# Three branch tiles loaded ahead of the gates, and a silu and two VectorE operations placed later, in a single-core decoder step

## What is computed

```python
q, k, v, iq, ik, iw, za, cu, zc, gt = split(x @ w_in)          # w_in: 2048 x 10832
# A: an indexer picks the top keys of each query, then sparse attention over them
sc   = sum_h relu(iq_h @ ik.T) * iw_h ; sel = top_k(sc)
attn = softmax(q @ k[sel].T * DH**-0.5 - slope * dist) @ v[sel]
# B: causal depthwise convolution, 31 taps
c    = depthwise_conv(ga * sigmoid(gb))
a_br = (attn * silu(za)) @ w_att_out                           # 1024 -> 2048
c_br = (silu(layer_norm(c)) * silu(zc)) @ w_conv_out           # 1024 -> 2048
mixed = sigmoid(gt[0]) * a_br + sigmoid(gt[1]) * c_br
y = layer_norm(ALPHA * x + mixed @ w_o)
```

## Time and profile before

| what | us |
|---|---|
| time, median of 3 runs (lowest to highest) | 1519.48 (1519.25 to 1519.65) |
| time of the profiled execution | 1517.25 |
| its span, first to last instruction | 1515.5 |
| PE busy in the span | 1492.2 (98%) |
| ACT / DVE / POOL busy | 888.6 / 680.6 / 668.5 |
| mean granted TensorE clock | 0.996 |

### The profile page before, as it was taken

How to read it: one execution, slowest core, us unless ns; L and a number is a source line. 1 busy time by engine, 2 the same in 40 slices (tenths; PEclk the granted TensorE clock), 3 DMA queues, 4 the chain that set the end, 5 groups by cost and what they waited for, 6 DMA issues and landing times.

```text
span 1515.5 us, 28644 instructions
## 1 busy us (share of the span) xinstructions
PE 1492.2 (98%) x11036; PEld 1166.2 (77%) x11036; DVE 680.6 (45%) x1444; ACT 888.6 (59%) x1218; POOL 668.5 (44%) x665
## 2 busy tenths in 40 slices
PE   9999999989999999999999999999999999999997
PEld 9955677877777877777777777877767777888885
DVE  4244677853241010118888888585123222121028
ACT  5798755656564565665566666769865665221120
POOL 5254433423332343365555565774444444333340
PEclk9999999999999999999999999999999999999999
DMA  7334343322333555633333333324354443732213
GB/s 266 84 89 115 88 121 85 92 80 79 107 100 112 162 144 141 198 96 99 84 84 84 84 88 101 102 57 135 115 154 130 133 147 115 253 122 82 80 60 125
DMA packets 246595, 174.11 MB, mean 115 GB/s; under 512 B 10449, under 2 KB 222897, under 8 KB 245631
## 3 DMA queue, kind: packets, MB, share of 16 engines
q1 hardware_dynamic: 241319, 162.00, 37.2%
q10 hardware_dynamic: 5160, 10.48, 1.9%
HBM read 156.31 MB, written 16.87 MB: 114 GB/s over the span
## 4 chain that ended last, share of the span: by engine, by line
PE 88%; ACT 5%; DVE 2%; POOL 2%; issue 1%; DMA 1%; DVEq 0%; SPq 0%; ACTq 0%
PE ps L1833 54%; PE ps L2207 12%; PE ps L1804 11%; PE ps L1905 3%; PE ps L1971 1%; PE ps L2100 1%; PE ps L1801 1%; ACT whi L958 1%; PE ps L1800 1%; PE ps L2090 1%; ACT scaled L957 1%; ACT squares L940 1%; DVE bias L1477 1%; ACT x L1013 1%; POOL wlo L824 1%
## 5 line engine op out<-in xcount | busy, mean ns | idle before, releaser
L1833 PE MATMUL ps<-x,whi 128*128 128x288 f16 (+2 forms) x4864 | 926.8, 291 | 0.0
L1833 PE MATMUL ps<-x,wlo 128*128 128x288 f16 (+2 forms) x2432 | 707.0, 291 | 0.0
L1833 PEld LDWEIGHTS ps<-x,whi 128*128 128x128 f16 x4864 | 472.0, 98 | 148.8 <-issue 8.4
L824 POOL TENSOR_TENSOR wlo<-scaled,whi 128x1024 f16<-128x1024 f32 x192 | 408.8, 2151 | 317.1 <-ACT whi L958 317.1
L1833 PEld LDWEIGHTS ps<-x,wlo 128*128 128x128 f16 x2432 | 238.1, 98 | 71.5
L957 ACT ACTIVATE scaled<-raw,few 128x1024 f32<-128x1024 f32 x192 | 219.5, 1143 | 20.2 <-POOL few L819 10.5
L958 ACT ACTIVATE whi<-raw,few 128x1024 f16<-128x1024 f32 x192 | 218.5, 1138 | 0.0
L947 ACT ACTIVATE few<-ps 128x1 f32<-128x1 f32 x96 | 16.3, 170 | 338.8 <-PE ps L1844 326.7
L2207 PE MATMUL ps<-b,whi 128*128 128x288 f16 x1024 | 190.1, 287 | 0.0
L940 ACT ACTIVATE squares<-raw 128x2048 bf16<-128x2048 f32 x95 | 180.4, 1898 | 6.2 <-DMA raw<-in_w_conv_out_dram 6.2
L1631 DVE SCALAR_TENSOR_TENSOR ps<-U,dwT,ps 128x512 f32<-128x512 f32 x232 | 175.2, 755 | 0.0
(11 more groups left out here) (308 smaller groups left out, 1485.5 us busy)
## 6 DMA issues: line engine op xcount, KB each, us to landing
raw<-in_w_in_dram SPq DMA_DIRECT2D x82, 1024.0 KB, 5.6
raw<-in_w_o_dram SPq DMA_DIRECT2D x16, 1024.0 KB, 5.0
both_gates<-gates_dram SPq DMA_DIRECT2D x16, 576.0 KB, 6.7
raw<-in_w_att_out_dram SPq DMA_DIRECT2D x16, 512.0 KB, 4.1
raw<-in_w_conv_out_dram SPq DMA_DIRECT2D x16, 512.0 KB, 5.4
gates_dram<-tmp_gate ACTq DMA_DIRECT2D x24, 288.0 KB, 2.1
vpage<-in_cache_v_dram SPq DMA_DIRECT2D x32, 128.0 KB, 2.7
kTs<-in_cache_k_dram SPq DMA_DIRECT2D x64, 64.0 KB, 1.9
```

What stands on the lines that cost most here:

```text
L824: ins = nc.gpsimd.tensor_tensor(wlo16[:, buf, c], scaled[:, c], whi16[:, buf, c], ALU.subtract)
L1833: ins = mm(ps[:, bank + half, 0:width], w[b][:, k, :], x16[:, k, x, t0 + half * width:t0 + (half + 1) * width], start=(k == 0 and m == 0), ...
```

## The change

Three edits, all of order alone; no instruction is added or removed.

- SP: branch tiles are loaded one at a time (`branch_tile(j)`) instead of in pairs. Three of them (0, 1, 2) are issued ahead of the waits for the stored gates and the operands, instead of two. After the gates of pair 0 the order is tile 3, tile 4, gates 1, tile 5, tile 6, gates 2, ..., tile 15, gates 7. So each of gates 1 to 6 now stands behind one more tile.
- POOL: `silu(N_G2 - 1)` stands behind `split_scaled(N_G2 + 1)` instead of ahead of it.
- DVE: the wait for v_hi, the v_lo subtraction and the q_last copy stand behind the four p_lo subtractions of group 0 (s == 1) instead of ahead of the softmax of group 0.

```diff
-            def branch_pair(i):
-                for b in range(2):
-                    n = N_BR + 2 * i + b
-                    buffer_free(n, scaled_only=True)
...
-            branch_pair(0)
+            def branch_tile(j):
+                n = N_BR + j
+                buffer_free(n, scaled_only=True)
+                for c, w in ((0, w_att_out), (1, w_conv_out)):
+                    sp.dma_start(raw[:, n % 2, c * DC:(c + 1) * DC].rearrange("p (k c) -> p k c", k=8),
+                                 w[:, j * P:(j + 1) * P].rearrange("(k p) c -> p k c", p=P)
+                                 ).then_inc(raw_here[n % 2], 16)
+
+            for j in range(3):
+                branch_tile(j)
 
             for s in gate_stored:
                 sp.wait_ge(s, 16 * 16)
...
             sp.wait_ge(xlo_ready, 3 * KC)
             for i in range(8):
                 if i:
-                    branch_pair(i)
+                    branch_tile(2 * i + 1)
+                    if i < 7:
+                        branch_tile(2 * i + 2)
...
-            silu(N_G2 - 1)
             for n in range(N_G2 + 1, N_BR):
                 split_scaled(n, 0.5)
+                if n == N_G2 + 1:
+                    silu(N_G2 - 1)
...
             dve.wait_ge(tile_taken, N_GT - C_OF + 2)
-            nc.vector.tensor_copy(q_last[:, :].rearrange("p (h t) -> p h t", h=HEADS), qT[:, :, 4 * P:LP]
-                                  ).then_inc(q_last_ready, 1)
-            dve.wait_ge(v_hi_ready, 1)
-            nc.vector.tensor_tensor(v_lo[:, :, :], kv[:, 0:4, KVH * DH:], v_hi[:, :, :].bitcast(F32), ALU.subtract
-                                    ).then_inc(v_lo_ready, 1)
             for s in range(GROUPS + 1):
                 if s >= 1:
...
                         nc.vector.tensor_tensor(lo, a, hi.bitcast(F32), ALU.subtract).then_inc(p_lo_ready, 1)
+                    if s == 1:
+                        dve.wait_ge(v_hi_ready, 1)
+                        nc.vector.tensor_tensor(v_lo[:, :, :], kv[:, 0:4, KVH * DH:], v_hi[:, :, :].bitcast(F32),
+                                                ALU.subtract).then_inc(v_lo_ready, 1)
+                        nc.vector.tensor_copy(q_last[:, :].rearrange("p (h t) -> p h t", h=HEADS), qT[:, :, 4 * P:LP]
+                                              ).then_inc(q_last_ready, 1)
                     dve.wait_ge(o_out, s)
```

## The result

| kernel | median us (lowest to highest) | profiled execution / its span | mean clock |
|---|---|---|---|
| before | 1519.47 (1519.25 to 1519.65) | 1517.25 / 1515.5 | 0.996 |
| changed | 1504.26 (1503.93 to 1504.5) | 1504.5 / 1502.7 | 0.998 |

The ratio is 0.9903, with a 95% interval of 0.9889 to 0.9917: 15.2 us less by the medians. I had forecast 1506.4 us, with a range of 1503.5 to 1511. The span of the profiled execution came down by 12.8 us; I had worked out 1502.4 for it.

The account below looks back on a forecast made before the run. PE was taken to bound the kernel, so only its idle time and slow clock could be won: 5.95 + 1.55 + 5.55 = 13.05 us off 1519.48 gives 1506.4 us, range 1503.5 to 1511.

Parts of the forecast that it names:

- What bounds: PE, busy for 1492.2 of 1515.5 us; the change aims at its waits of 4.1, 1.55 and 3.8 us.
- Attention: PE's 4.1 us wait at the transposes goes, with 1.5 us of slow clock and 0.35 at the transposes: 5.95 us.
- v_lo and q_last behind p_lo: On DVE at group 0, both end before they are needed; v_lo has at least 5 us of cover.
- Silu: At gate tile N_G2 + 1, PE's 1.55 us wait ahead of the norm matmul goes, with no clock tail.
- Branch tiles: Behind tile N_BR, PE's 3.8 us wait goes and 1.75 us of slow clock with it: 5.55 us.
- (a): Softmax of group 0 takes over q_last's and v_lo's port waits: 8.2 us saved, 1511.3 us; chance 5%.
- (b): Branch wait returns one tile later, up to 3 us, a long one with 1.75 us tail: 1508 to 1511; chance 9%.
- (c): Gates 1 to 6 land after DVE wants them, at all six pairs: slower, 1523.2 us; chance 2%.
- (d): PE's idle time turns up elsewhere in pieces, so under 3 us are won: 1517 us; chance 3%.
- the slow clock behind the two long waits: PE's tiles behind the 4.1 and 3.8 us waits run slow, costing 1.5 and 1.75 us.
- the 2.2 us between profile and median: The kernel before's median lies 2.2 us above its profiled time; the same saving was taken from 1519.48 us.
- the case where all goes as planned: All three waits go: 1506.4 us with 81%, its own range 1504.5 to 1508.5.

Follow-up runs that it names:

- silu alone: The kernel before with only the last silu on POOL moved behind the next tile's scaling: 1516.43 us, ratio 0.9988.
- q_ahead: The changed kernel with the q_last copy put back ahead of the softmax of group 0, v_lo staying behind: 1505.09 us.

## Why the prediction was right, point by point

- **What bounds.** PE's waits were the right list: the three that the change aims at went, the rest stayed, and no new one came.
- **Attention.** I had the softmax ending between 302.9 and 303.6 with PE at 303.7; it ended at 303.4 in a profile that is 0.6 us later, 0.8 us before PE. ACT's exponentials started at 299.7 and followed each other every 0.39 us; the cover was the one that I had worked out. The transposes took 0.93 us (forecast 0.9) and the tile 11.76.
- **v_lo and q_last behind p_lo.** p_lo began at 307.2 and v_lo ended at 309.7 (forecast 309.1 to 311.2, or 309.7 to 311.8 with the 0.6). v_lo took 1.21 us, as it started ahead of POOL's subtraction, which took 4.92 us instead of 4.23. q_last then took 2.16 behind it.
- **Silu.** The scale operations started at 1006.5 and the squares were there at 1014.45 (7.9 us; forecast 8.0), 2.1 us before PE (cover forecast 2.2). The 1.55 us went; silu alone measured 1.2. The silu then delayed the next scale operations by 1.9 us, as forecast (2 us): their norm was there at 1017.0 and they started at 1018.87. But I had that delay pass on to the squares (cover 1.6), and it didn't reach ACT, which was busy with a table load and the square root until 1019.9:

```profile
1017.50 1.40 POOL L868 TENSOR_TENSOR zc<-tmp_tanh,zc 128x576 f32<-128x576 f32 x1
1018.87 0.22 POOL L818 TENSOR_SCALAR fewint<-few 128x1 int32<-128x1 int32 x1
```
```profile
1018.01 1.28 ACT L1314 ACT_TABLE_LOAD   x1 [0.39 <-ACT tmp_tanh L1289]
1019.31 0.68 ACT L1314 ACTIVATE c_rstd<-c_sum 128x576 f32<-128x576 f32 x1
```

The squares were there at 1026.3, 3.1 us before PE.
- **Branch tiles.** The squares were there 2.4 us before PE (forecast 2.4), and POOL's low part of N_BR + 2 ended at 1122.2, 1.7 us before PE (forecast cover 1.6). No wait took the place of the one removed.
- **Rivals.** (a) is out: the scores and maxima ran at their old pace (0.29 us each) under POOL's subtraction of 295.7 to 299.9. The scalings (L1524) started at 300.4, behind it. They did not run beside it at group 1 of the kernel before either (331.4 against 330.2), so my "the same operations at group 1" covered only the first half of the softmax, and no trace here shows a scaling beside POOL's subtraction. (b) is out by the rows above. (c) is a real mechanism and turns the sign when the gates are a tile later still; in the changed kernel it isn't near. (d) is out: the parts add up.
- **The term that was mis-sized** is the slow clock behind the two long waits. I put 1.85 us (0.35 of it at the transposes) and 1.75 us from one profiled execution; other executions show 2.8 and 2.9 to 3.0. I took the 2.2 us between profile and median for a difference that would stay. As far as the profiles of the single edits show, it was mostly this, and it went with the waits: so 15.2 us beside one sample of the kernel before and 13.6 beside another. It also put the measured 1504.26 just below the 1504.5 to 1508.5 that I gave to the case where all goes as planned. It lies in the full range of 1503.5 to 1511 by 0.8 us, and that lower edge was a margin, not something that I had worked out.

## What to carry to other kernels

When one engine is busy for 98% of the span, list its waits, and for each ask what stands ahead of the late work on the releasing queue but is due later; moving that costs nothing while its own reader is far off, and the profile of before gives both times. A long wait of PE also has a slow stretch behind it whose length differs from run to run, so a saving that removes it can be larger than one profile shows. A short DVE operation that takes microseconds beside GpSimd work may be waiting, as here, and can cost its neighbour time too (0.7 to 1.0 us here).

## What the runs showed of the hardware that I had not expected

- The slow stretch behind a wait of 3.8 to 4.3 us cost 1.75 to 3.0 us (tiles of 13.51, 14.66 and 14.75 us instead of 11.78). What differed was when the clock fell: during the wait, or 1.4 us after PE had started again. Behind waits of 0.6, 1.0, 1.55 and 2.0 us the profiles show none (tiles of 11.84, 11.76, 11.76, 11.76); behind 2.7 us (a tile of 13.43), 2.8 and 3.3 us (clock 0.94 and 0.89 over the next two tiles) they do.
- A DVE subtraction of two SBUF tiles took 1.21 us when it started ahead of a POOL subtraction and 3.1 us when it started just behind the beginning of one, and in both places POOL lost time too (4.92 and 5.22 us instead of 4.23). Started in the middle of POOL's first half (`q_ahead`) it took 2.06 us.
